# Last eight chunks of a phase token half by token half, the next phase entered the same way, in a one-core encoder layer

## What is computed

```python
h = h + 0.5 * rms_norm(swiglu_ffn(rms_norm(h, g1), w1_in, w1_out), g1_post)   # 2048 -> 2*5632 -> 2048
h = h + rms_norm(hybrid_mixer(rms_norm(h, g2), ...), g2_post)
h = h + 0.5 * rms_norm(swiglu_ffn(rms_norm(h, g3), w2_in, w2_out), g3_post)

def rms_norm(x, g):
    return x * rsqrt(mean(x * x, axis=-1) + 1e-6) * g
def swiglu_ffn(x, w_in, w_out):
    g, u = split(x @ w_in, 2)
    return (silu(g) * u) @ w_out
def hybrid_mixer(u, ...):          # one projection u @ w_in gives q, k, v of A and B and two gates
    m = sigmoid(ga + bga) * (A(q, k, v) @ w_up_a) + sigmoid(gb + bgb) * (B(q, k, v) @ w_up_b)
    return m @ w_out               # A: windowed attention; B: neighbourhood attention with bias table rpb_b
```

## Time and profile before

| | |
|---|---|
| median of 3 runs | 2099.9 us (2097.09 to 2100.04) |
| the profiled execution's own time | 2096.38 us |
| its span in the profile | 2094.6 us |
| busy share of the span | PE 99%, PEld 82%, DVE 57%, ACT 51%, POOL 2% |
| chain that ended last | PE 97%, DVE 1%, DMA 1% |
| DMA | 400.84 MB, mean 191 GB/s |
| mean granted clock of PE | 0.995 |

### The profile page before, as it was taken

How to read it: one execution, slowest core, us unless ns; L and a number is a source line. 1 busy time by engine, 2 the same in 40 slices (tenths; PEclk the granted TensorE clock), 3 DMA queues, 4 the chain that set the end, 5 groups by cost and what they waited for, 6 DMA issues and landing times.

```text
span 2094.6 us, 27070 instructions
## 1 busy us (share of the span) xinstructions
PE 2066.4 (99%) x9268; PEld 1709.3 (82%) x9268; DVE 1192.3 (57%) x1856; ACT 1075.7 (51%) x1848; POOL 48.6 (2%) x83
## 2 busy tenths in 40 slices
PE   9999999999999989999999999999999999999997
PEld 7888888888888878888888888788888888888886
DVE  6555555555555565566666666565555555555554
ACT  7454544454444454445555555565555555544443
POOL 1000000000000011110000000000000000000000
PEclk9999999999999999999999999999999999999999
DMA  8666666666655657775555556466666666665553
GB/s 300 191 193 193 189 204 193 197 185 211 194 193 193 193 158 223 220 214 175 158 159 160 180 189 211 142 202 191 184 195 190 190 184 190 190 210 194 194 192 131
DMA packets 205387, 400.84 MB, mean 191 GB/s; under 512 B 13944, under 2 KB 13944, under 8 KB 204928
## 3 DMA queue, kind: packets, MB, share of 16 engines
q1 hardware_dynamic: 200976, 388.05, 59.5%
q0 software_dynamic: 4336, 11.82, 2.6%
HBM read 395.87 MB, written 3.92 MB: 191 GB/s over the span
## 4 chain that ended last, share of the span: by engine, by line
PE 97%; DVE 1%; DMA 1%; ACT 0%; issue 0%; POOL 0%; DVEq 0%; SPq 0%; POOLq 0%; ACTq 0%
PE acc L855 31%; PE acc L857 31%; PE acc L856 31%; PE tp L890 1%; PE tp L946 1%; PE tp L969 1%; PE tp L871 0%; PE tp L957 0%; DVE h L631 0%; PE tp L936 0%; DMA raw<-in_w_in 0%; DVE tmp L682 0%; DMA raw<-in_ffn_w_in 0%; DVE WL L556 0%; DVE tmp L684 0%
## 5 line engine op out<-in xcount | busy, mean ns | idle before, releaser
L556 DVE TENSOR_TENSOR WL<-raw,WH 128x512 fp32r<-128x512 f32 x1456 | 1000.6, 692 | 863.6 <-ACT WH L352 859.6
L352 ACT ACTIVATE WH<-raw 128x512 fp32r<-128x512 f32 x1456 | 912.1, 631 | 966.2 <-PE acc L857 951.6
L855 PE MATMUL acc<-WH,XH 128*128 128x512 f32 x2080 | 822.7, 396 | 3.2 <-DVE WL L556 3.2
L857 PE MATMUL acc<-WH,XL 128*128 128x512 f32 x2080 | 811.8, 390 | 0.0
L856 PE MATMUL acc<-WL,XH 128*128 128x512 f32 x2080 | 811.0, 390 | 0.0
L855 PEld LDWEIGHTS acc<-WH,XH 128*128 128x128 f32 x2080 | 391.8, 188 | 82.7 <-issue 3.8
L857 PEld LDWEIGHTS acc<-WH,XL 128*128 128x128 f32 x2080 | 391.3, 188 | 82.7
L856 PEld LDWEIGHTS acc<-WL,XH 128*128 128x128 f32 x2080 | 391.9, 188 | 79.0
L855 PE MATMUL acc<-WH,MH 128*128 128x512 f32 x704 | 274.0, 389 | 0.0
L857 PE MATMUL acc<-WH,ML 128*128 128x512 f32 x704 | 273.9, 389 | 0.0
L856 PE MATMUL acc<-WL,MH 128*128 128x512 f32 x704 | 273.9, 389 | 0.0
(11 more groups left out here) (89 smaller groups left out, 572.2 us busy)
## 6 DMA issues: line engine op xcount, KB each, us to landing
raw<-in_ffn_w_in SPq DMA_DIRECT2D x352, 512.0 KB, 4.2
raw<-in_ffn_w_out SPq DMA_DIRECT2D x176, 512.0 KB, 4.5
raw<-in_w_in SPq DMA_DIRECT2D x136, 512.0 KB, 4.2
raw<-in_w_out SPq DMA_DIRECT2D x32, 512.0 KB, 4.3
raw<-in_w_up_a SPq DMA_DIRECT2D x16, 512.0 KB, 4.0
raw<-in_w_up_b SPq DMA_DIRECT2D x16, 512.0 KB, 4.5
gates<-in_b_gate POOLq DMA_DIRECT2D x16, 256.0 KB, 5.2
xT<-in_x_turned SPq DMA_DIRECT2D x4, 512.0 KB, 8.0
```

What stands on the lines that cost most here:

```text
L352: act.activation(WH[:, c % WS, :], raw[:, c // 2 % RAW, c % 2, :], ACT.Copy).then_inc(hi_ready, 1)
L556: dve.tensor_tensor(WL[:, c % WS, :], raw[:, c // 2 % RAW, c % 2, :], WH[:, c % WS, :].bitcast(F32), ALU.subtract).then_inc(lo_ready, 1)
L855: pe.matmul(a, hi[:, tok], WH[:, w, :], start=first, stop=False)
L857: mm = pe.matmul(a, lo[:, tok], WH[:, w, :], start=False, stop=last)
```

## The change

Six things are changed.

1. In the last block of FFN out and of the out projection, the last eight chunks (`SKEW`) run for token half 0 first, which counts up `half_done`, then for half 1 (`skewed_block`). Squares, mean square, root, post gain and update of `h` are made per half (`half_squares`, `mean_square_of`, `inverse_root_of`, `half_times_post_gain`, `scaled`), and `update_h` runs through the four pieces of half 0, then those of half 1.
2. The new phase's first block begins the same way (`enter`): chunks 0 to 7 for half 0, chunks 0 to 7 for half 1, chunks 8 to 15 for both. `h` is turned in 24 units (`unit_tile`): units 0 to 7 are half 0 of groups 0 to 7, units 8 to 15 half 1 of them, 16 to 23 both halves of groups 8 to 15. The first four stand in PE's list ahead of the last chunk of half 1 of the old phase.
3. Since the eight chunks at either side are used twice, a second ring of eight slots (`EH`, `EL`, in space of `MH`, `ML` that is free then) holds chunks -8 to -1 and 8 to 15 around a boundary, and ACT and DVE split eight chunks of the new phase ahead, with up to 16 chunks in hand.
4. ACT takes all eight `h_square` at the end of the entry block, where they stood between groups 4 and 11.
5. POOL issues the four table reads of a head one by one, four chunks apart, and the gate bias loads in the gate phase; each head has its own semaphore, and DVE's `mask_bias` stands a block later.
6. The final stores go by token half.

The core of the diff:

```diff
+def in_second_ring(c):
+    return any(n - WS <= c < n or n + WS <= c < n + 2 * WS for n in (C_QKV, C_F2IN))
+def slots_of(c):
+    return 2 * WS if any(n - WS <= c < n + 2 * WS for n in (C_QKV, C_F2IN)) else WS
+def unit_tile(u):
+    if u < 2 * SKEW:
+        return u % SKEW, range(u // SKEW, u // SKEW + 1)
+    return u - SKEW, range(TT)
...
@@ gpsimd @@
-            inverse_root(1)
             inverse_root(2)
             for hd in range(B_H):
-                pool.wait_ge(chunk_done, C_QKV + hd * DC + 12)
                 for r in range(ROWS):
+                    pool.wait_ge(chunk_done, C_QKV + hd * DC + 12 + 4 * r)
...
-                    pool.dma_start(dst, src).then_inc(rpb_landed[hd % 2], 16)
-                pool.wait_ge(chunk_done, C_QKV + hd * DC + DC + 4)
...
+                    pool.dma_start(dst, src).then_inc(rpb_landed[hd], 16)
+            for b in range(GATE_BLOCKS):
+                pool.wait_ge(chunk_done, C_GATE + b * DC + 2)
...
@@ scalar @@
-                    act.wait_ge(chunk_done, c - WS + 1 + more)
+                    act.wait_ge(chunk_done, c - slots_of(c) + 1 + more)
...
+            def enter(n, chunk, b_last):
+                for c in range(WS):
                     split_hi(chunk + c)
+                half_squares(b_last, 2 * n - 1, 0)
+                for c in range(8, 11):
+                    split_hi(chunk + c)
+                for u in range(4):
+                    normed_hi(n, u)
+                half_squares(b_last, 2 * n - 1, 1)
...
+                split_hi(chunk + 15)
+                for j in range(OUT_BLOCKS):
+                    for t in range(TT):
+                        h_square(n, j, t)
+                    normed_hi(n, 20 + j)
...
@@ vector @@
+            def enter(n, chunk, b_last, gp, weight):
+                for c in range(WS):
+                    split_lo(chunk + c)
+                mean_square_of(2 * n - 1, 0)
+                half_times_post_gain(b_last, n - 1, gp, weight, 0)
+                split_lo(chunk + 8)
+                scaled(b_last, n - 1, 0)
+                for j in range(OUT_BLOCKS):
+                    update_h(n - 1, 0, j)
+                for u in range(4):
+                    normed_lo(n, u)
+                mean_square_of(2 * n - 1, 1)
+                half_times_post_gain(b_last, n - 1, gp, weight, 1)
+                for u in range(4, 6):
+                    normed_lo(n, u)
+                scaled(b_last, n - 1, 1)
+                for j in range(OUT_BLOCKS):
+                    update_h(n - 1, 1, j)
+                    for u in range(2 * j + 6, 2 * j + 8):
+                        if j < 3:
+                            normed_lo(n, u)
...
@@ tensor @@
+            def skewed_block(c0, b, chunks, hi, lo, n):
+                acc_free(b)
+                for c in range(chunks - SKEW):
+                    chunk(c0 + c, b, hi[:, c, :], lo[:, c, :], c == 0, False)
+                for c in range(chunks - SKEW, chunks):
+                    pe.wait_ge(lo_ready, c0 + c + 1)
+                    mm = half(c0 + c, b, 0, hi[:, c, :], lo[:, c, :], c == 0, c == chunks - 1)
+                mm.then_inc(half_done, 1)
+                for c in range(chunks - SKEW, chunks):
+                    if n and c == chunks - 1:
+                        for u in range(4):
+                            turn_h(n, u)
+                    half(c0 + c, b, 1, hi[:, c, :], lo[:, c, :], c == 0, c == chunks - 1).then_inc(chunk_done, 1)
...
+            def enter(n, c0, b):
+                units = DC + UNITS * (n - 1)
+                acc_free(b)
+                for c in range(SKEW):
+                    pe.wait_ge(xt_lo, units + c + 1)
+                    pe.wait_ge(lo_ready, c0 + c + 1)
+                    half(c0 + c, b, 0, XH[:, c, :], XL[:, c, :], c == 0, False)
+                    if c % 2:
+                        turn_h(n, c + 3)
                         turn_h(n, c + 4)
+                for c in range(SKEW):
+                    pe.wait_ge(xt_lo, units + SKEW + c + 1)
+                    half(c0 + c, b, 1, XH[:, c, :], XL[:, c, :], c == 0, False).then_inc(chunk_done, 1)
+                    if c % 2:
+                        turn_h(n, SKEW + c + 3)
+                        turn_h(n, SKEW + c + 4)
```

More of the change, by code:

```diff
@@ L55 @@
 WS = 8
-AHEAD = WS - 1
+SKEW = 8
+UNITS = 24
 RPB_FIRST = 32
@@ L308, in _ @@
             pool.dma_start(gp_ffn[:, :], ffn1_post_g.broadcast_to([P, D])).then_inc(post_gain_landed, 16)
+            for t in range(TT):
+                inverse_root_of(1, t)
             pool.wait_ge(chunk_done, C_QKV)
@@ L340, in _ @@
             pool.dma_start(gp_ffn[:, :], ffn2_post_g.broadcast_to([P, D])).then_inc(post_gain_landed, 16)
-            inverse_root(5)
+            for t in range(TT):
+                inverse_root_of(5, t)
         @block.scalar
@@ L421, in ffn @@
+            def ffn(c_in, c_out, b_in, b_out, m0, norm, n):
+                if n == 0:
+                    for c in range(DC):
+                        first_hi(c)
+                        split_hi(c_in + c)
+                        if c >= 14:
+                            h_square(0, 0, c - 14)
                     for c in range(DC):
@@ L637, in ffn @@
+            def ffn(c_in, c_out, b_in, b_out, m0, norm, n):
                 if n == 0:
+                    for c in range(DC):
+                        first_lo(c)
+                        split_lo(c_in + c)
                     for c in range(DC):
@@ L796, in _ @@
                     split_lo(C_GATE + g * DC + c)
+                    if c == 4 and g == 0:
+                        mask_bias(B_H - 1)
                     if c == 2 and g:
@@ L847, in _, with half @@
+            ffn(C_F2IN, C_F2OUT, B_F2IN, B_F2OUT, M_F2, 4, 2)
+            for t in range(TT):
+                mean_square_of(5, t)
+                half_times_post_gain(B_END - 1, 2, gp_ffn, 0.5, t)
+                scaled(B_END - 1, 2, t)
+                for j in range(OUT_BLOCKS):
+                    update_h(2, t, j)
         @block.tensor
         def _(pe):
+            def half(c, b, t, hi, lo, first, last):
+                a, tok = acc[:, 2 * (b % 2) + t, :], slice(t * P, (t + 1) * P)
+                pe.matmul(a, hi[:, tok], weight_hi(c), start=first, stop=False)
+                pe.matmul(a, hi[:, tok], weight_lo(c), start=False, stop=False)
+                return pe.matmul(a, lo[:, tok], weight_hi(c), start=False, stop=last)
@@ L849, in chunk @@
             def chunk(c, b, hi, lo, first, last, more=0):
                 pe.wait_ge(lo_ready, c + 1 + more)
-                w = c % WS
                 for t in range(TT):
-                    a, tok = acc[:, 2 * (b % 2) + t, :], slice(t * P, (t + 1) * P)
-                    pe.matmul(a, hi[:, tok], WH[:, w, :], start=first, stop=False)
-                    pe.matmul(a, hi[:, tok], WL[:, w, :], start=False, stop=False)
-                    mm = pe.matmul(a, lo[:, tok], WH[:, w, :], start=False, stop=last)
+                    mm = half(c, b, t, hi, lo, first, last)
```

266 lines of the change are left out of this document (151 added, 115 removed).

## The result

The changed kernel takes 2078.4 us (median of 4 runs, 2078.0 to 2078.8) where the kernel before took 2098.5 in the same job (median of 4, 2096.5 to 2100.0). The ratio is 0.9906, with a 95% interval of 0.9894 to 0.9919: 20.1 us or 0.94% less. Two of these four runs of before lie near 2100, which is rare: against the median of all 72 runs of the kernel before in this document, 2097.15, it is 18.8 us or 0.90%. In the profiled executions the difference is 17.56 us (2096.38 to 2078.82, span 2094.6 to 2077.0).

The account below looks back on a forecast made before the run. TensorE was busy 99% of the span, so time could only come from its standing still or running slowly. Sum 7.6 + 6.2 − 0.1 + 0.0 + 3.25 = 16.95 us; 2099.9 − 16.95 = 2083.0, range 2078.5 to 2089.

Parts of the forecast that it names:

- T: The moment at which half 0 of a phase's last block is complete; forecast times at a boundary count from it.
- Boundaries: First boundary (FFN 1 to QKV) and second: 7.6 and 6.2 us given back, before 0.1 for the table load.
- table load: Second boundary: ScalarE's 1.28 us load ahead of the second block's first split, ready T+31.1, wanted 31.0; cost 0.1 us.
- Rival A: Entry blocks still wait (unit 0 no slack, unit 8 0.7 us), 1 to 3 us each: 2085 to 2090; chance 0.17.
- Rival B: Weights run short in QKV's block 1 or where the ring fills, 1 to 3 us: 2084 to 2086; chance 0.13.
- C: Clock falls to the 1.2 GHz level in the reordered stretches: slower, 2104, or 2134 with two whole entry blocks; chance 0.03.
- D: Nothing won at the boundaries, half 1's chain open in place of half 0's; only the end won: 2096; chance 0.02.
- The step that failed: From the profiled execution to the runs' median, 3.5 us above it: 2099.9 − 16.95 = 2083.0.
- QKV's wait: TensorE's wait for `tmp` in QKV's block 1: 2.2 us, no change; bounds 1.4 to 4.8, 0.9 won to 2.5 lost.
- The end: Behind the last matmul: one square in place of two, four updates in place of eight; 3.25 off 11.5 us.
- 4.46 standing, 3.1 for six microseconds at half clock: First boundary: 7.6 us too many, 4.46 of TensorE standing and 3.1 for six microseconds at clock 0.50.
- the tables' spacing: QKV's block 1: by the Trainium skill's rules, spreading the table reads would win 0.4 us in place of nothing.

Follow-up runs that it names:

- The first experiment: The kernel before, unedited, timed against itself and profiled once more: 2098.0 us, ratio 1.0001.
- e3: The kernel before with 34 transposes that nothing needs filling TensorE's standstill at each boundary: 2094.9 us, ratio 0.9986.
- e4: The kernel before with 18 matmuls of 512 columns that nothing needs filling TensorE's standstill at each boundary: 2094.9 us, ratio 0.9986.
- e5: The changed kernel with a head's four table reads in one burst and the gate-bias loads in QKV, as before: 2078.2 us.
- e6: The kernel before with table reads one by one, gate-bias loads in the gate phase, mask a block later: 2097.3 us, ratio 1.0002.

## Why the prediction was right, and where it was off

**The mechanism was right.** TensorE stood still at both boundaries for a chain of small operations, and the change puts that chain under matmuls. From T, the timeline has squares, updates, transposes, phase end and unit 8 within 0.1 us of the forecast, the mean square and the root 0.1 and 0.5 sooner; the updates gained nothing by that, since the split in VectorE's list ended when the forecast had the root. VectorE is done with the eighth split ahead at 731.8, 1.4 us ahead of T where some 3 were forecast:

```profile
730.49 1.29 DVE L633 TENSOR_TENSOR WL<-raw,WH 128x512 fp32r<-128x512 f32 x2 [0.96 <-ACT WH L401]
```

That was enough, since ScalarE waited for nothing more before the squares. TensorE's waits at `tp<-ident,h` are gone. The entry block ends at T+31.2, forecast 31.0. Boundaries: 7.43 and 6.02, forecast 7.6 and 6.1 with the table load. That load cost nothing: at the second boundary it ran from 1359.64 to 1360.92, and VectorE was through block 1's first split at about 1362.3, 0.8 ahead of the block's start at 1363.07. The prediction's own terms say so too: 28.2 + 1.28 + 0.63 + 0.69 is 30.8 and not 31.1, so the 0.1 was a slip. Rival A (unit 0 without slack) did not come, but with 1.36 us less cover it does, by 0.8 us of waiting and 1.0 of time a boundary: there was some half microsecond to spare. Rival B did not come either: behind the program's start TensorE waits for no weight split. Rivals C and D are out: clock 1.00, and both chains covered.

**The sum against its own execution was right too**: 2096.4 − 16.95 = 2079.4, measured 2078.8. Its terms against the traces: boundaries 13.7 forecast, 13.45 measured; QKV 0.0 and 1.07; end 3.25 and 3.88; and a start 0.90 longer that no step spoke of. That it came within 0.6 us is in part luck: QKV and the end gave 1.7 more than booked, and the slow start of that execution took 0.90 back.

**The step that failed is the last**: "The runs' median lies 3.5 above that execution, so its like is 2099.9 − 16.95 = 2083.0." Its base was a median of three runs: 2097.1, 2099.9 and 2100.0. The kernel before ran 72 times in all: the median is 2097.15, 62 runs lie at or below 2098.98, and ten at or above 2099.90, with none between. Two of the three were of the ten. So 2.75 of the 4.6 us are this base (2099.9 − 2097.15), bad luck with a small sample. The other 1.8 is that from 2097.15 to 2078.4 are 18.8 us, where the sum had 16.95: QKV and the end were booked 1.07 and 0.63 too low, the boundaries 0.25 too high, and 0.35 is less than the medians of the jobs differ by. Had the step taken the typical run, the forecast would have been 2080.2.

Why ten of 72 runs take 3 us longer is open, since none of them was profiled. The first experiment's execution, 2098.05, is not one of them; it shows one thing that lengthens a run and that the change takes away, 1.48 us of half clock behind the wait for `tmp`. The runs lie 3.5 to 5 us apart for the kernel before in every job, 3.9 with the end changed alone, 2.2 and 3.4 with the boundaries filled (in the second the clock fell behind the wait for `tmp`: 13.86 in QKV's column), 0.9 with the change, 2.9 with the change and only four chunks of cover, and 0.2 with no stop over 0.4 us after the start. (These are 4 to 33 runs each, so the spreads are rough.) That fewer stops make the runs lie closer fits this, and is not shown.

**QKV's wait, 1.2 in place of 2.2.** The step "I take 4.5 ... 2.3 + 1.2 − 1.3 = 2.2" was off in two of its figures. The chain of the changed kernel (start, us, what) has the piece:

```profile
761.76 1.20 DVE WL L633 x2
...
762.98 4.17 DMA raw<-in_w_in
...
768.45 1.42 DVE tmp L803 x2
...
769.91 1.09 PE tp L1098 x8
```

It is issued 1.44 ahead of the block's start at 764.42, not 0.8, and it lands in 4.17, not 4.5. It is issued sooner because ScalarE came free at 760.87, T+27.6 and not T+28.2; in its timeline the second square of a pair starts 0.62 behind the first, where 0.72 was booked for each:

```profile
759.28 0.62 ACT L428 ACTIVATE tmp<-h 128x512 f32<-128x512 f32 x1
...
759.90 0.62 ACT L428 ACTIVATE tmp<-h 128x512 f32<-128x512 f32 x1
...
760.51 0.46 ACT L412 ACTIVATE XH<-tp,gainT 128x256 fp32r<-128x256 f32 x1
...
760.87 4.39 ACT L401 ACTIVATE WH<-raw 128x512 fp32r<-128x512 f32 x8
```

With both, 2.2 − 0.64 − 0.33 = 1.23, the wait seen. The bound "0.9 won" was 0.2 too narrow.

**The end, 3.9 in place of 3.25.** One square less was booked at 0.6. From the last matmul's slot to the first update it is 2.0 us now (2069.42 to 2071.43), and was 3.0 (2083.08 to 2086.1): 1.0 less. The mean square starts 0.7 sooner, behind one square and no longer behind the post gain, and from there to the first update it is 1.10 where it was 1.36, with a root of 0.54 where it was 0.71. The prediction has the post gain's new place at the boundary and leaves it out here. The updates take 2.74 where they took 5.39, 2.65 less as forecast, and 0.3 less lies behind the last update:

```profile
2070.33 0.16 DVE L657 TENSOR_REDUCE ms<-ssq 128x1 f32<-128x4 f32 x1 [1.56 <-ACT tmp L462]
...
2071.43 2.74 DVE L711 SCALAR_TENSOR_TENSOR h<-fg,rstd,h 128x512 f32<-128x512 f32 x4
```

**The clock.** The price "4.46 standing, 3.1 for six microseconds at half clock" was right as a sum, but its parts are not worth that alone: without the half clock only 2.1 comes back there, and 0.7 at the second boundary, as e3 and e4 show. For the whole change this made no difference; for the edit that fills a standstill it halves the gain.

The Trainium skill (TensorE: Matmul & The Clock Gate, Part 4: PE-mode transpose) has it that transposes do not count as activity for the clock. The filled standstills speak against it, for the fp32 transposes of this kernel: 34 transposes and 18 matmuls gave the same excess to 0.01 us, at full clock. Its rule on issuing engines and on rows under 512 B (DMA: Bandwidth & Descriptors, Issuing engines are not separate DMA queues, and Specifications) gave 0.4 us for the tables' spacing in the prediction, where my own sum had nothing. The rule's sharing may be there (0.30 and 0.25 in QKV's column, with the doubts told at e5 and e6), but the step from it does not hold: the tables do not explain all of 5.83 over 4.2, since without the burst the piece took 5.60. What else made it slow in the kernel before is open.

## What to carry to other kernels

Where a phase's end is a chain of small operations on other engines, split the last chunks by the half that the chain can start on, and count the cover in matmul time: here 5.9 us, with the transposes, covered a chain whose last update ends at 5.2 and whose first operand is there at 5.8, and two chunks less already cost 1.0 a boundary. Subtract a sum worked out from one profiled execution from that execution; before adding the distance to a median, look how many runs it rests on (three here, two of them rare ones), and ask whether the change removes what makes the runs differ. Price a lost clock by filling the standstill, since what runs slowly may hide the next wait.

## What the hardware showed that I had not expected

Transposes alone kept TensorE's clock up: 34 of them (3.88 us) in a standstill; and 30 ahead of the first matmul raised it before that started, where 16 followed by 2.7 us of standing did not. A stop of 2.2 to 2.3 us was followed by half clock in one execution of the same program and not in another, and of five stops of 2.1 to 2.4 us in front of QKV's transposes three were; behind stops of 1.0 to 1.7 us it was not seen in any trace here. The start's half clock lasted until 11.1 in one execution of before and until 13.2 in another. And with the clock up from the start TensorE waits 1.08 us for weights, with the DMA engines full (a share of 1.03, 408 GB/s).
